# Second attention in fp32: one full-precision product of probabilities and values becomes three rounded ones, with the sums copied by VectorE

## The chip, the cores and the metric

The kernel runs on one core of one Trainium2 chip. The time is that of the whole kernel in device microseconds. Engines: PE is TensorE (PEld its weight loads), ACT ScalarE, DVE VectorE, POOL GpSimd, and SP the queue that issues nearly all DMAs.

## The reference, cut to what matters

The program is two transformer-like blocks, one after the other. The change lies in the attention of the second block (`mla_mixer`), 8 heads, 1024 queries, 1040 keys (16 of them "meta" keys), with a mask by chunks of 64 positions:

```
s = jnp.einsum('bqhd,bkhd->bhqk', qb, k).astype(jnp.float32) * scale
mask = cid[None, :] <= qc[:, None]
s = jnp.where(mask[None, None], s, neg)
p = jax.nn.softmax(s, axis=-1).astype(v.dtype)
return jnp.einsum('bhqk,bkhd->bqhd', p, v)
...
return o * jax.nn.silu(z)
```

Everything is fp32. After it `h = h + y @ w_out` ends the program.

## The kernel before

Each engine has one program, written out by hand; engines meet only through semaphores. `Steps` counts the steps that an engine has finished, and `w.wait_ge(*act_at.at("exp", h, u))` makes an engine wait for one of them. An engine works strictly in its order, so whatever stands behind a waiting instruction waits as well.

Nearly all matrix products of the kernel are made in a split form: an fp32 operand is rounded to fp32r (its high part), the remainder (fp32 minus high part) is rounded as well (its low part), and high by high, low by high and high by low are summed in PSUM. The product of probabilities and values is the exception: there both operands are plain fp32, and each such matmul runs as two passes (`x2` in the trace).

`attend_pe` goes through 8 heads of 14 units. A unit `(hf, x, c0)` is one block `x` of 128 keys (the last has 16) against one half `hf` of the queries, without the masked columns: 512 columns wide in 6 units of a head, 448, 320 and 192 in two each, and 64 in two (one with 16 keys). In each unit PE does

1. `scores(h, u)`: three fp32r products into one of three "unit" banks (0 to 2),
2. `values(j - 2)`: the fp32 product of the unit two before into the bank of its half (3 or 4), of `vm` (values of two heads with a block of ones between them, so that the sums of probabilities come out beside the result) and `pt`,
3. a step of preparation for the next head: turns of queries and keys (units 0 to 3), the 14 products for the row maxima (`max`, two in each of units 4 to 10) and the turn of the maxima (unit 11), through banks 5 to 7. In head 7 the preparation is gone and the input `y` of the last projection is turned instead.

ACT takes the exponential of a unit into one of four buffers `pt`, copies queries and keys to their high parts `qh` and `kh`, and copies sums and results from PSUM (`summed`: `den`, `og`). DVE makes the low parts `ql` and `kl`, the maxima (TENSOR_REDUCE), the reciprocals of the sums (`inverse`, 4 for each half of a pair of heads), and writes the shift of the next head into `qh`. POOL only multiplies result, gate and reciprocal (`z o` and `y`), 4 instructions for each pair of heads. `kl` has to be made before its bank can take a maxima product, and the shift before the next head's scores.

The last projection (`output_pe`, 8 panels of 128 columns, `pe_dense`) takes its input parts `k` in the order 6, 7, 2, 3, 4, 0, 1, 5. For each, `y_high_act` writes the high part into `XH`, `y_low_dve` the low part into `XL`. Parts 6, 7, 2, 3, 4 are split during head 7 (`early`), parts 0, 1 and 5 of the first half at its end. Part 5 is the result of the last pair of heads.

Of the kernel before, what the change touches and what calls it, by code (L numbers as in the profile page):

```python
# [15 lines left out]
NB = 8  # L16
NMETA = 16
# [128 lines left out]
def build(nc, ap, ctx):  # L146
# [3369 lines left out]
    pts = [X(f"pt{i}", 37888 + 2048 * i, [512]) for i in range(4)]  # L3516
# [27 lines left out]
    def values_of(h, x):  # L3544

        return vm[0:n_keys(x), x, h // 2, h % 2:h % 2 + 2, :]
# [102 lines left out]
    def attend_pe(pe, w):  # L3649
# [10 lines left out]
        def values(j):  # L3660
            h, u = j // nu, j % nu
            hf, x, c0 = units[u]
            if x == 0:
                take(w, "values", ("o", h, hf), (act_at, ("o", h, hf)))
            w.wait_ge(*act_at.at("exp", h, u))
            w.wait_ge(*pool_la.at("ones"))
            pe.matmul(tile("o", h, hf)[:, c0:512], values_of(h, x), pts[j % 4][0:n_keys(x), 0:512 - c0], start=(x == 0), stop=(x == last_x[hf])  # L3667
                      ).then_inc(*pe_at.up("values", j))

        for h in range(8):  # L3670
            for u in range(nu):
                scores(h, u)
                if nu * h + u >= 2:
                    values(nu * h + u - 2)
                if h < 7:
                    for step in prepare[u]:
                        prepare_pe(pe, w, h + 1, *step)
                elif u < 4:
                    y_turn_pe(pe, w, *early[u])
        values(8 * nu - 2)  # L3680
        values(8 * nu - 1)

    def attend_act(act, w):
        def summed(h, hf):
# [5 lines left out]
            act.activation(den[hf][a:a + 64, :], p[b:b + 64, :], ACT.Copy).then_inc(*act_at.up("den", h, hf))  # L3690
            act.activation(og[hf][a:a + 64, :], p[a:a + 64, :], ACT.Copy).then_inc(*act_at.up("o", h, hf))

        for h in range(8):
            for u in range(nu):
                hf, x, c0 = units[u]
                j = nu * h + u
                w.wait_ge(*pe_at.at("unit", h, u))
                if j > 3:
                    w.wait_ge(*pe_at.at("values", j - 4))
                act.activation(pts[j % 4][0:n_keys(x), 0:512 - c0], tile("unit", h, u)[0:n_keys(x), 0:512 - c0], ACT.Exp).then_inc(*act_at.up("exp", h, u))  # L3700
                if u == 2 and h > 0:
# [392 lines left out]
```

## Time and profile before

| what | value |
|---|---|
| median of 3 runs | 1920.88 us (1919.63 to 1922.67) |
| the profiled execution's own time | 1921.68 us |
| its span | 1919.9 us |
| second attention, first score product to first product of the last projection | 1656.3 to 1829.25 us |
| last projection to the end | 1829.25 to 1919.9 us |
| PE busy over the span | 1858.6 us (97%) |
| DVE, ACT, POOL busy over the span | 1188.0, 783.2, 553.2 us |

An average over the span says nothing of a stage: the change lies in 173 us of it, so those are read by head, by wait and by single instructions. A start time minus the one before it is the price of a matmul on PE; the durations shown of matmuls overlap.

### The profile page before, as it was taken

The page shows a single profiled execution, that of the slowest core. Times are in us where ns is not written, and L with a number is a line of the kernel's source. Part 1 is how long each engine was busy: PE and PEld are TensorE (multiplying, and loading weights), DVE is VectorE, ACT ScalarE, POOL GpSimd, SP SyncE. Part 2 cuts the span into 40 slices and gives each one's busy share as a digit, 9 for nine tenths or more (in the row PEclk, how much of TensorE's full clock was granted, in tenths as well). Part 3 has the DMA queues.
Part 4 walks back from the last instruction along what each step waited for, and adds up shares of the span by engine and source line. Part 5 has one row for each costly group of instructions (what it writes and reads, how often), then busy time and mean ns, then how long its engine had stood idle before and what let it go on. Part 6 is the DMA issues. An engine that isn't in the chain of part 4 may idle for free.

```text
span 1919.9 us, 24216 instructions
## 1 busy us (share of the span) xinstructions
PE 1858.6 (97%) x9462; PEld 1511.5 (79%) x9462; DVE 1188.0 (62%) x1805; ACT 783.2 (41%) x1404; POOL 553.2 (29%) x555
## 2 busy tenths in 40 slices
PE   8999999899988999999999998999999999999999
PEld 5788788666777888887888887879988897676687
DVE  6678445555788676767877877455435347666642
ACT  6765323455543333433333354452211137455520
POOL 0120026440537666620000024551523125111100
PEclk9999999999999999999999999999999999999999
DMA  4143433300314535469555500113101313411131
GB/s 161 44 148 105 148 89 105 110 23 34 132 56 159 175 127 180 138 263 398 210 191 189 206 1 29 47 59 132 45 23 34 121 45 140 129 34 34 45 131 66
DMA packets 110042, 216.27 MB, mean 113 GB/s; under 512 B 37528, under 2 KB 42904, under 8 KB 105832
## 3 DMA queue, kind: packets, MB, share of 16 engines
q1 hardware_dynamic: 109640, 214.49, 32.8%
q8 instruction: 75, 1.23, 0.3%
q14 instruction: 39, 0.32, 0.1%
q10 hardware_dynamic: 288, 0.22, 0.0%
HBM read 153.82 MB, written 60.87 MB: 112 GB/s over the span
## 4 chain that ended last, share of the span: by engine, by line
PE 74%; DVE 10%; ACT 6%; POOL 4%; issue 3%; DMA 2%; SPq 0%; DVEq 0%; POOLq 0%; ACTq 0%
PE ps L362 10%; PE ps L363 9%; PE ps L364 9%; PE ps L1949 5%; PE ps L1951 5%; PE ps L1950 5%; PE ps L2337 5%; PE ps L2338 5%; PE ps L2339 5%; PE ps L3667 4%; PE ps L379 3%; PE ps L707 2%; ACT sc L1503 1%; PE ps L3568 1%; PE ps L3656 1%
## 5 line engine op out<-in xcount | busy, mean ns | idle before, releaser
L362 PE MATMUL ps<-xh,whi 128*128 128x512 f32 (+2 forms) x1160 | 458.7, 395 | 8.8 <-DVE wlo L331 5.1
L363 PE MATMUL ps<-xl,whi 128*128 128x512 f32 (+2 forms) x1160 | 443.8, 383 | 0.0
L364 PE MATMUL ps<-xh,wlo 128*128 128x512 f32 (+2 forms) x1160 | 442.9, 382 | 0.0
L362 PEld LDWEIGHTS ps<-xh,whi 128*128 128x128 f32 x1160 | 220.5, 190 | 58.2 <-issue 11.5
L364 PEld LDWEIGHTS ps<-xh,wlo 128*128 128x128 f32 x1160 | 220.5, 190 | 40.0
L363 PEld LDWEIGHTS ps<-xl,whi 128*128 128x128 f32 x1160 | 220.6, 190 | 33.2
L1949 PE MATMUL ps<-oph,wsh 128*128 128x512 f32 x448 | 177.2, 396 | 11.2 <-DVE stu L2067 6.0
L2337 PE MATMUL ps<-dnh_b,dnh_a 128*128 128x512 f32 x448 | 175.2, 391 | 4.7 <-DVE dn_b L2363 4.7
L1950 PE MATMUL ps<-opl,wsh 128*128 128x512 f32 x448 | 176.4, 394 | 0.0
L1951 PE MATMUL ps<-oph,wsl 128*128 128x512 f32 x448 | 176.3, 393 | 0.0
L2338 PE MATMUL ps<-dn_b,dnh_a 128*128 128x512 f32 x448 | 174.9, 390 | 0.0
L2339 PE MATMUL ps<-dnh_b,dn_a 128*128 128x512 f32 x448 | 174.8, 390 | 0.0
L2354 ACT ACTIVATE dnh_a<-dnr_a 128x2048 fp32r<-128x2048 f32 x28 | 53.7, 1918 | 188.9 <-PE ps L2339 174.9
L319 ACT ACTIVATE whi<-wraw 128x1024 fp32r<-128x1024 f32 x71 | 74.3, 1046 | 135.6 <-PE ps L364 124.3
L331 DVE TENSOR_TENSOR wlo<-wraw,whi 128x1024 fp32r<-128x1024 f32 x70 | 95.1, 1359 | 55.6 <-ACT whi L319 55.5
L1949 PEld LDWEIGHTS ps<-oph,wsh 128*128 128x128 f32 x448 | 85.5, 191 | 30.6 <-DVE stu L2067 6.5
L2337 PEld LDWEIGHTS ps<-dnh_b,dnh_a 128*128 128x128 f32 x448 | 84.5, 189 | 23.1 <-DVE dn_b L2363 5.4
L1951 PEld LDWEIGHTS ps<-oph,wsl 128*128 128x128 f32 x448 | 85.4, 191 | 17.9
L1950 PEld LDWEIGHTS ps<-opl,wsh 128*128 128x128 f32 x448 | 85.5, 191 | 17.8
L2339 PEld LDWEIGHTS ps<-dnh_b,dn_a 128*128 128x128 f32 x448 | 84.4, 188 | 17.7
L2338 PEld LDWEIGHTS ps<-dn_b,dnh_a 128*128 128x128 f32 x448 | 84.5, 189 | 17.4
L3667 PE MATMUL ps<-pt,vm 128*128 128x512 f32 (+4 forms) x224 | 89.8, 485 | 0.9 <-ACT pt L3700 0.9
(516 smaller groups left out, 3397.7 us busy)
## 6 DMA issues: line engine op xcount, KB each, us to landing
wraw<-panels SPq DMA_DIRECT2D x70, 512.0 KB, 3.6
dnr_b<-ff_d SPq DMA_DIRECT2D x28, 1024.0 KB, 7.6
dnr_a<-down SPq DMA_DIRECT2D x28, 1024.0 KB, 5.1
ff_d<-st SPq DMA_DIRECT2D x64, 256.0 KB, 5.9
ff_d<-stt SPq DMA_DIRECT2D x48, 256.0 KB, 5.9
upx<-up SPq DMA_DIRECT2D x16, 512.0 KB, 3.9
upy<-up SPq DMA_DIRECT2D x16, 512.0 KB, 5.5
hT<-x SPq DMA_DIRECT2D x8, 512.0 KB, 5.1
```

The lines of the kernel that those rows point to most:

```text
L319: act.activation(whi[b][:, 0:n], raw[b][:, 0:n], ACT.Copy).then_inc(*act_w.up(i))
L331: dve.tensor_tensor(wlo[b][:, 0:n], raw[b][:, 0:n], whi[b][:, 0:n].bitcast(F32), ALU.subtract).then_inc(*dve_w.up(i))
L362: pe.matmul(out, h, xh[:, xk, c0:c1_], start=(n == 0), stop=False)
L363: pe.matmul(out, h, xl[:, xk, c0:c1_], start=False, stop=False)
L364: mm = pe.matmul(out, l, xh[:, xk, c0:c1_], start=False, stop=(n == nk - 1))
L1949: pe.matmul(out, h, opH[i][:, j], start=(i in FIRST_UP and j == 0), stop=False, skip_group_check=i not in FIRST_UP)
L1950: pe.matmul(out, h, opL[i][:, j], start=False, stop=False, skip_group_check=i not in FIRST_UP)
L1951: mm = pe.matmul(out, l, opH[i][:, j], start=False, stop=(j == 3), skip_group_check=i not in FIRST_UP)
L2337: pe.matmul(out, h[:, j, cs], xh[:, j], start=(i in (1, 5, 6, 7) and j == 0), stop=False, skip_group_check=i in (2, 3, 4))
L2338: pe.matmul(out, h[:, j, cs], xl[:, j], start=False, stop=False, skip_group_check=i in (2, 3, 4))
L2339: mm = pe.matmul(out, l[:, j, cs], xh[:, j], start=False, stop=(j == 3), skip_group_check=i in (2, 3, 4))
L3667: pe.matmul(tile("o", h, hf)[:, c0:512], values_of(h, x), pts[j % 4][0:n_keys(x), 0:512 - c0], start=(x == 0), stop=(x == last_x[hf])).the ...
```

## The change

The product of probabilities and values is made of three fp32r products as the others are.

- Values: `value_high_act` (ACT) and `value_low_pool` (POOL) split the values of each pair of heads, `vhs`/`vls`, two buffers. The first pair is split at the start of the stage, pairs 1 to 3 in units 5 (ACT) and 6 (POOL) of heads 0, 2 and 4.
- Probabilities: ACT takes the exponential twice, once into `ph` (fp32r, six buffers) and once into `pt` (fp32, now three buffers). POOL subtracts them into `pl` (four buffers). One `pt` is free again when POOL has subtracted, one `ph` and `pl` when PE has done the third product.
- PE: `values_high(j - 2)` (two products), and `values_low(j - 4)` (the third) follow the scores of a unit.
- `summed` moves from ACT to DVE, and to units 4 and 12 (was 2 and 7). The reciprocals of a pair of heads now all stand in the even head behind it, units 0 to 3 and 5 to 8 (were in units 10 to 13 of the odd head and 3 to 6 of the even one).
- POOL's `gated` and `divided` stand between its subtractions, and for the last pair behind all of them.
- In head 7 `early` starts at unit 4 (was 0). All loads of `hr` (the last sum's other operand) are issued after the attention; three stood ahead of it. They also come behind a weight panel's load.

```diff
+    def value_high_act(act, w, c):
+        if c == 0:
+            w.wait_ge(*pe_la.at("mz", 3, HALF2))
...
+        for n, bs in value_parts:
+            act.activation(vhs[c % 2][0:n, bs, 0:3:step, :], vm[0:n, bs, c, 0:3:step, :], ACT.Copy).then_inc(*act_at.up("vh", c, n))
...
+    def value_low_pool(pool, w, c):
+        if c == 0:
+            w.wait_ge(*pool_la.end())
...
+        for n, bs in value_parts:
+            w.wait_ge(*act_at.at("vh", c, n))
+            pool.tensor_tensor(vls[c % 2][0:n, bs, 0:3:step, :], vm[0:n, bs, c, 0:3:step, :], vhs[c % 2][0:n, bs, 0:3:step, :].bitcast(F32), ALU.subtract).then_inc(*pool_at.up("vl", c, n))
...
+        def values_high(j):
...
+            w.wait_ge(*act_at.at("exp high", h, u))
+            w.wait_ge(*pool_at.at("vl", c, NMETA))
...
+        def values_low(j):
...
+            w.wait_ge(*pool_at.at("p low", j))
...
-                if nu * h + u >= 2:
-                    values(nu * h + u - 2)
+                if j >= 2:
+                    values_high(j - 2)
+                if j >= 4:
+                    values_low(j - 4)
...
+                act.activation(p_high(j)[0:n, 0:512 - c0], p, ACT.Exp).then_inc(*act_at.up("exp high", h, u))
+                if j > 2:
+                    w.wait_ge(*pool_at.at("p low", j - 3))
+                act.activation(pts[j % 3][0:n, 0:512 - c0], p, ACT.Exp).then_inc(*act_at.up("exp", h, u))
...
+        for n in range(4):
+            inverse(3, 0, n)
+        summed(7, 1)
+        for n in range(4):
+            inverse(3, 1, n)
         for k in (0, 1, 5):
             if k > 0:
                 w.wait_ge(*pe_at.end())
             y_low_dve(dve, w, k, 0)
-        for n in range(4):
-            inverse(3, 1, n)
...
+                w.wait_ge(*act_at.at("exp", h, u))
+                if j > 3:
+                    w.wait_ge(*pe_at.at("values", j - 4))
+                pool.tensor_tensor(p_low(j)[0:n, 0:512 - c0], pts[j % 3][0:n, 0:512 - c0], p_high(j)[0:n, 0:512 - c0].bitcast(F32), ALU.subtract
+                                   ).then_inc(*pool_at.up("p low", j))
```

What the change makes of two places in the programs. First DVE, from the first split of `y` in head 7 to the splits for the second half of the projection, before:

```order
L3646 TENSOR_TENSOR xl<-ps,xh 128x512 x4
L3646 TENSOR_TENSOR xl<-zf_305,xh 128x512 x6
L3718 RECIPROCAL den_353<-den_353 128x128 x4
L3646 TENSOR_TENSOR xl<-yb,xh 128x512 x2
L3646 TENSOR_TENSOR xl<-zf_305,xh 128x512
L3718 RECIPROCAL den_354<-den_354 128x128 x4
L3646 TENSOR_TENSOR xl<-yb,xh 128x512 x2
```

and now:

```order
L3687 TENSOR_TENSOR xl<-ps,xh 128x512 x4
L3687 TENSOR_TENSOR xl<-zf_305,xh 128x512 x4
L3772 COPY den_375<-ps 64x512
L3773 COPY og_373<-ps 64x512
L3687 TENSOR_TENSOR xl<-zf_305,xh 128x512 x2
L3778 RECIPROCAL den_375<-den_375 128x128 x4
L3772 COPY den_376<-ps 64x512
L3773 COPY og_374<-ps 64x512
L3778 RECIPROCAL den_376<-den_376 128x128 x4
L3687 TENSOR_TENSOR xl<-yb,xh 128x512 x2
L3687 TENSOR_TENSOR xl<-zf_305,xh 128x512
```

Behind the splits of `early`, two copies and four reciprocals of the second half now stand ahead of the low parts of `yb` (parts 0 and 1), which were ahead of them.

Then POOL in units 3 to 8 of head 4, where before it had only four multiplications (`zf<-zf,og` and `zf<-zf,den`) in the whole head; now:

```order
L3826 TENSOR_TENSOR pl_357<-pt_347,ph_353 128x192
L3826 TENSOR_TENSOR pl_354<-pt_345,ph_348 128x64
L3816 TENSOR_TENSOR zf_305<-zf_305,den_375 128x512
L3826 TENSOR_TENSOR pl_355<-pt_346,ph_349 128x512
L3826 TENSOR_TENSOR pl_356<-pt_347,ph_350 128x512
L3587 TENSOR_TENSOR vl_370<-vm,vh_368 128x8x2x64
L3587 TENSOR_TENSOR vl_370<-vm,vh_368 16x2x64
L3826 TENSOR_TENSOR pl_357<-pt_345,ph_351 128x512
L3810 TENSOR_TENSOR zf_305<-zf_305,og_374 128x512
L3826 TENSOR_TENSOR pl_354<-pt_346,ph_352 128x512
```

The four multiplications and the split of the next pair's values stand between the subtractions on whose result PE's third product waits.

## Rows read from the trace of the kernel before

**Rows 1.** The page, busy time, share of the span and instructions.
```profile
PE 1858.6 (97%) x9462; PEld 1511.5 (79%) x9462; DVE 1188.0 (62%) x1805; ACT 783.2 (41%) x1404; POOL 553.2 (29%) x555
```
**Rows 2.** Busy time by stretch: heads 2, 5, 7.
```profile
1700.20:1722.20 22.00, 21.70 (x104) 15.40 (x103) 16.46 (x29) 11.51 (x23) 3.82 (x3) 1.00 0.16 37
...
1765.90:1787.80 21.90, 21.63 (x104) 15.32 (x102) 11.92 (x22) 11.47 (x24) 1.27 (x1) 1.00 0.00 1
...
1809.70:1829.30 19.60, 19.60 (x93) 13.73 (x91) 11.10 (x15) 14.97 (x31) 1.72 (x2) 1.00 0.00 1
```
**Rows 3.** Waits in the stretch 1655 to 1835 (total, times, longest).
```profile
ACT pt L3700 <- PE ps L3658: 69.2, 67, 1.7
...
PE ps L3568 <- DVE kl L3593: 1.9, 7, 0.3
```
**Rows 4.** The chain that ended last, in order of time.
```profile
1690.29 0.86 PE ps L3667 x2
```
**Rows 5.** Timeline of PE: start, duration, line.
```profile
1755.36 0.39 PE L3656 MATMUL ps<-qh,kh 120*128 120x512 f32 x1
1755.59 0.39 PE L3657 MATMUL ps<-ql,kh 96*128 96x512 f32 x1
...
1764.47 0.28 PE L3657 MATMUL ps<-ql,kh 96*128 96x192 f32 x1
1764.58 0.27 PE L3658 MATMUL ps<-qh,kl 96*128 96x192 f32 x1
```
**Rows 6.** POOL by line and form: busy us, mean ns.
```profile
L1630 POOL TENSOR_TENSOR xl<-gat,xh 128x512 fp32r<-128x512 f32 x8 | 10.2, 1280 | 26.7 <-ACT xh L1616 26.7
...
L3125 POOL TENSOR_TENSOR cnv<-cnv,f 128x1024 f32<-128x1024 f32 x2 | 4.9, 2456 | 10.0 <-DVE f L2808 10.0
...
L1198 POOL TENSOR_TENSOR tk<-tk,c 128x64 f32<-128x64 f32 x8 | 2.6, 323 | 0.0
```
**Rows 7.** Timeline of the start of the stage.
```profile
1657.09 1.06 ACT L3252 ACTIVATE zf<-zf 128x1024 f32<-128x1024 f32 x1 [5.39 <-DVE zf L2808]
...
1657.71 1.04 POOL L3383 CAST qh<-aq 24x1024 fp32r<-24x1024 f32 x1
...
1660.11 1.12 PE L3667 MATMUL ps<-pt,vm 128*128 128x512 f32 x2 [0.89 <-ACT pt L3700]
```
**Rows 8.** Timeline of PE around a long wait in an earlier stage.
```profile
608.04 0.80 PE L1949 MATMUL ps<-oph,wsh 128*128 128x512 f32 x1 [6.03 <-DVE stu L2067]
608.63 0.63 PE L1950 MATMUL ps<-opl,wsh 128*128 128x512 f32 x1
...
613.32 0.43 PE L1949 MATMUL ps<-oph,wsh 128*128 128x512 f32 x1
```
**Rows 9.** DVE by line and form: copy from PSUM.
```profile
L1548 DVE COPY sc<-ps 128x512 f32<-128x512 f32 x14 | 9.7, 690 | 2.6 <-PE ps L379 2.4
```
**Rows 10.** Timeline of ACT in head 7.
```profile
1818.09 0.60 ACT L3700 ACTIVATE pt<-ps 128x512 f32<-128x512 f32 x1 [0.35 <-PE ps L3658]
...
1818.59 0.62 ACT L3641 ACTIVATE xh<-zf 128x512 fp32r<-128x512 f32 x1
...
1820.76 0.59 ACT L3690 ACTIVATE den<-ps 64x512 f32<-64x512 f32 x1
...
1821.38 0.59 ACT L3691 ACTIVATE og<-ps 64x512 f32<-64x512 f32 x1
```
**Rows 11.** Timeline of the end of head 7 and the start of the projection.
```profile
1825.41 3.38 DVE L3718 RECIPROCAL den<-den 128x128 f32<-128x128 f32 x4
...
1828.82 2.39 DVE L3646 TENSOR_TENSOR xl<-yb,xh 128x512 fp32r<-128x512 f32 x2
1828.87 1.78 POOL L3747 TENSOR_TENSOR zf<-zf,den 128x512 f32<-128x512 f32 x1 [5.54 <-DVE den L3718]
```
**Rows 12.** Timeline in head 2: DVE and POOL at the same time.
```profile
1702.87 0.75 DVE L3598 SCALAR_TENSOR_TENSOR ql<-ps,vec,qh 96x512 fp32r<-96x512 f32 x1
...
1702.92 1.28 POOL L3747 TENSOR_TENSOR zf<-zf,den 128x512 f32<-128x512 f32 x1 [9.40 <-DVE den L3718]
```
**Rows 13.** The page, DMA issues: KB each, us to landing.
```profile
hT<-x SPq DMA_DIRECT2D x8, 512.0 KB, 5.1
```

More of the change, by code:

```diff
@@ L3689, in summed @@
                 w.wait_ge(*pool_at.at("y", h // 2 - 1, hf))
[L3690 to L3701, printed above, removed]
-                    summed(h - 1, 1)
-                if u == 7:
-                    summed(h, 0)
-                if h < 7:
-                    for step in prepare[u]:
-                        prepare_act(act, w, h + 1, *step)
-                elif u < len(early):
-                    y_high_act(act, w, *early[u])
-        for k in (0, 1, 5):
-            y_high_act(act, w, k, 0)
-        summed(7, 1)
-    def attend_dve(dve, w):
+            dve.tensor_copy(den[hf][a:a + 64, :], p[b:b + 64, :]).then_inc(*dve_at.up("den", h, hf))
+            dve.tensor_copy(og[hf][a:a + 64, :], p[a:a + 64, :]).then_inc(*dve_at.up("o", h, hf))
         def inverse(c, hf, n):
             d = den[hf][:, 128 * n:128 * n + 128]
-            w.wait_ge(*act_at.at("den", 2 * c + 1, hf))
+            w.wait_ge(*dve_at.at("den", 2 * c + 1, hf))
             dve.reciprocal(d, d).then_inc(*dve_at.up("inverse", c, hf, n))
@@ L3724, in attend_dve @@
                         prepare_dve(dve, w, h + 1, *step)
[L3725 to L3730 removed]
+                if h > 0 and h % 2 == 0 and u < 4:
+                    inverse(h // 2 - 1, 0, u)
+                if u == 4 and h > 0:
+                    summed(h - 1, 1)
+                if h > 0 and h % 2 == 0 and 5 <= u < 9:
+                    inverse(h // 2 - 1, 1, u - 5)
+                if u == 12:
+                    summed(h, 0)
+                if h == 7 and 4 <= u < 4 + len(early):
+                    y_low_dve(dve, w, *early[u - 4])
+        for n in range(4):
[3 more added lines that the diff above has]
+            inverse(3, 1, n)
         for k in (0, 1, 5):
@@ new lines, in divided @@
+        def divided(c, hf):
+            z = zf2[:, c, 512 * hf:512 * hf + 512]
+            w.wait_ge(*dve_at.at("inverse", c, hf, 3))
+            w.wait_ge(*pool_at.at("z o", c, hf))
+            pool.tensor_tensor(z, z, den[hf][:], ALU.mult).then_inc(*pool_at.up("y", c, hf))
+        value_low_pool(pool, w, 0)
+        for h in range(8):
+            for u in range(nu):
+                hf, x, c0 = units[u]
+                j, n = nu * h + u, n_keys(x)
+                w.wait_ge(*act_at.at("exp", h, u))
[3 more added lines that the diff above has]
+                                   ).then_inc(*pool_at.up("p low", j))
+                if h % 2 == 0 and h < 6 and u == 6:
+                    value_low_pool(pool, w, h // 2 + 1)
+                if h > 0 and h % 2 == 0:
+                    if u == 0:
+                        gated(h // 2 - 1, 0)
+                    if u == 4:
+                        divided(h // 2 - 1, 0)
+                    if u == 7:
+                        gated(h // 2 - 1, 1)
+                    if u == 10:
+                        divided(h // 2 - 1, 1)
@@ L3864, in sp_program @@
         w.wait_ge(*st_h1.end())
-        for n in range(3):
-            sp.dma_start(hr[n][:], h1_d[n]).then_inc(*ld_hr[n].up())
         sp_weights(sp, w, OUT0 + 3)
         w.wait_ge(*pe_at.end())
-        for n in range(3, 8):
+        for n in range(8):
             sp.dma_start(hr[n][:], h1_d[n]).then_inc(*ld_hr[n].up())
```

105 lines of the change are left out of this document (77 added, 28 removed).

## The prediction

> **What bounds the kernel now.** I read the page first. PE is busy 97% of the span [rows 1], so the first question is whether PE is also the limit inside the stretch that is changed. The busy time by stretch says yes: of the 22.0 us of head 2 PE is busy 21.70, of the 21.9 of head 5 21.63, and in head 7 it never rests [rows 2]. A head takes 21.9 us, and in it ACT works 11.5 us, DVE 16.5 in even heads (those with reciprocals) and 11.9 in odd ones, POOL at most 3.8. The waits confirm it from the other side: ACT stood 69.2 us in all for PE's scores, while the largest wait of PE's products was 1.9 us in 7 times, for `kl` [rows 3]. So every microsecond taken from PE here counts until another engine is the limit, and the other three have, per head of 21.9, about 10 (ACT), 5 to 10 (DVE) and 18 (POOL) us to give. The change takes little from PE and gives much to the three.
>
> **The change part by part.** All in us, against the profiled execution.
>
> *PE's work.* A full fp32 product of values (two passes, 512 columns) takes 0.86 on the chain [rows 4]. An fp32r product of 512 columns comes 0.23 after the one before it, one of 192 columns 0.11 [rows 5], so a narrow one costs no less than its weight load. Three products cost 0.70 (512 columns), 0.33 (192) and 0.33 (64). Scaled with the columns from 0.86, the fp32 product costs 0.77, 0.54, 0.33, 0.22 for 448, 320, 192, 64. Between the rows, three fp32r products cost 0.62 and 0.44 for 448 and 320. A head saves 6 x 0.16 + 2 x 0.15 + 2 x 0.10 + 2 x 0 - 2 x 0.11 = 1.3, eight heads **10.3**. PE then needs 20.6 for a head.
>
> *The start.* PE's first product of values began at 1660.1, when ACT's first exponential was done, after a wait of 0.9 [rows 7]. Now it needs the low values of the first pair. POOL is busy until 1658.75 (its copy at 1657.71), ACT ends its gate at 1658.15 [rows 7] and then splits 1536 elements, about 1.4 if 512 take 0.5 [rows 10], until about 1659.6. POOL's subtraction of 1536: a two-operand POOL instruction takes 1.28 for 512 and 2.46 for 1024 [rows 6], so 3.6, and 0.6 for the 16 meta rows (192 elements, between 0.32 for 64 and 1.28). PE can go on at about 1663.9: **+3.8**, an idle PE of some 4.8.
>
> *What idleness does to the clock.* At 601.6 to 608.0 PE waited 6.03 us, and the 12 matmuls after it came 0.43 apart, 5.28 for what takes 2.8 at 0.23 [rows 8]: that is the lower of the two clock levels, 1.2 in place of 2.4 GHz, and it cost 2.5. For the shorter wait at the start I take **+1.0**, since PE's slower products there partly run while it would wait for POOL anyway.
>
> *POOL in the heads.* 14 subtractions in a head, the same operation as the first line of [rows 6]: 6 x 1.31 + 2 x (1.17 + 0.88 + 0.59) + 2 x 0.30 = 13.8, with a few hundredths between two. That is under 20.6. But head 0 has the split of the second pair in one piece behind unit 6, 3.6 + 0.6 = 4.2, while a low part has only about two units of slack (it is made some 3 us after the scores, and used four units later, 5.9 us): I take **+1.7** for PE in units 11 to 13. Heads 2 and 4 have 13.8 + gaps 0.5 + four multiplications 5.2 + a split of 1024 and 128 elements 2.8 = 22.3: more than PE's 20.6, so the saving is gone, **+1.7** each. In heads 3 and 5 ACT's copies of keys stand behind exponentials that wait for POOL's backlog, and `kl`, for which PE already waits, comes later: **+1.25** each. Their bounds are 0 and about 2.6, the wait of one long POOL piece handed on twice.
>
> *DVE in the heads.* Four copies of 64x512 from PSUM: 0.69 each by a copy of the same length [rows 9], 2.8 a head; and four more reciprocals (0.845 each, [rows 11]) in even heads: 16.5 + 2.8 + 3.4 = 22.7 of durations, about a tenth less by their distance on the engine. So even heads are at DVE's limit too. In heads 2 and 4 this lies beside POOL's; in head 6, without a split, I take **+0.7**. In sum +6.6 in heads 1 to 6; odd head 1 follows a head without reciprocals and costs nothing.
>
> *ACT in the heads.* +14 exponentials, about 5.5 by a spacing of 0.50 at 512 columns, -2.4 for the sums: 14.6 of 20.6. Not the limit, except in head 7: there each unit is two exponentials and a split of `y`, 3 x 0.50 = 1.5 [rows 10], against PE's 1.4, and DVE's low parts read two SBUF operands while POOL subtracts: **+1.3**, that is, head 7 keeps its 18.7 to 19.
>
> *The end.* This is the largest term. DVE's order, as the part on the change shows it, puts behind the attention: one or two low parts 1.2, eight reciprocals 6.8, two copies 1.2, and only then the low part 0, 0.7: about 9.9 us after PE's last value product. PE has five of eight parts ready, 15 products, 3.5. It waits 6.4. Next to POOL's multiplications the low parts of `yb` took 2.39 for two in place of 1.38 [rows 11], so low parts 0 and 1 each come later by up to 0.5: **+7.0**. Before, the same low parts came at 1828.82 and nothing waited. That wait is as long as the one of [rows 8] and is followed by full-width products: **+2.5** for the clock.
>
> *The loads of `hr`.* Issued behind the split of a panel, some 13 us after the attention, 5.1 us to landing [rows 13]. DVE's first evacuation waits for it, but PE has four banks, two panels or 22 us of products plus its own stall, so it is hidden with some 8 us to spare. If it were not, each us late is a us.
>
> Sum: -10.3 + 3.8 + 1.0 + 1.7 + 6.6 + 1.3 + 7.0 + 2.5 = **+13.6**. On the profiled execution's 1921.7 (its span 1919.9 and 1.8 around it) that is 1935.3; this execution is 0.8 above the median of its three runs, so I forecast **1934.5**.
>
> **A rule weighed against the rows.** While POOL's multiplication ran at 1702.92 in its usual 1.28, DVE made a `ql` (one operand in PSUM, one in SBUF) at 1702.87 in its usual 0.75 [rows 12]: no contention. With two SBUF operands there was some: POOL 1.78 and DVE 2.39 for two [rows 11]. The sum goes by these rows.
>
> The Trainium skill ("SBUF — State Buffer", section "SBUF: two separate sides") says that DVE with two SBUF inputs and GpSimd reading SBUF share one port pair under an exclusive lock, and that the one who comes second is blocked for the whole instruction of the other. The trace agrees in which instructions collide. By the rule in full, a low part at the end could wait for a whole 1.3 us multiplication, which would make the sum some 0.7 larger.
>
> **The rivals.**
> 1. *The heads keep up* (0.15). The lag of POOL is absorbed by the buffers, and heads 1 to 6 run at PE's 20.6. For it: the mean POOL work over two heads is 18, below 20.6. Against it: a low part has only four units before PE needs it, and a `pt` three. Then 13.6 - 6.6 - 1.7 = +5.3: 1926.
> 2. *ACT becomes the limit of the middle* (0.15). Two activations that read the same bank might not overlap: `den` and `og`, from one bank, were 0.62 apart and not 0.50 [rows 10]. Then a unit's pair costs 0.12 to 0.24 more, 2 to 3 a head, and copies of keys come later by as much in every head; about +1 a head over my sum: +20, 1941.
> 3. *POOL slower beside DVE* (0.12). If the reductions and copies of DVE also stretched POOL, say by the 15% between 1.28 and the 1.5 or so of a half overlapped pair, POOL has 25 in heads 2 and 4 and 4.8 at the start: +6.6 more, 1941.
> 4. *The other side: a full fp32 product costs PE more than its 0.86* (0.04), in that the next weight load can't run under its second pass. If 0.2 us of each of the 112 were hidden in the products around them, 22.4 more would be saved: 13.6 - 22.4 = -8.8, 1912. It decides from 13.6 / 112 = 0.12 us a product on. Against it: the starts of 0.23 in [rows 5] leave no such room.
> 5. *The wait at the end does not come* (0.04), because DVE's reciprocals get done before PE is: they can't start before DVE has the last `early` splits, so only if head 7 were held up by others long enough. Then -9.5 and head 7 longer: about +4, no change or slightly slower.
>
> The main case has 0.50.
>
> **How the numbers follow.** A measurement of this kernel tells some 0.2%, 3.8 us. Main case, own range 1930 to 1940 (start 3 to 5, heads 3 to 10, end and clock 7 to 11). The range goes from rival 1 to rivals 2 and 3: 1925 to 1945. Faster holds rival 4, 0.04; within 0.2% the fifth and the edge of the first, 0.06; slower the rest, 0.90.
>
> **What the new profile would show.** Products of values: 336 of fp32r, three in 0.70. PE idle once for 4 to 5 us at about 1660, then once for 6 to 7 us some 3.5 us after the first product of the last projection, followed by 7 to 12 products 0.43 apart. Head periods: about 26 for head 0, 20.5 for head 1, 22 for 2 and 4, 21.5 for 3 and 5. POOL busy some 120 us more, nearly without rest in heads 2 and 4. Wrong would be: heads of 20.6 throughout (POOL and DVE are hidden), heads of 23 or more (rivals 2, 3), or a projection that starts without a wait.

## The result: 0.8% slower, and the profile after

The changed kernel takes 1936.54 us (median of 4 runs, 1933.89 to 1937.24) against 1920.51 for the kernel before (4 runs). The ratio is 1.008, with a 95% interval from 1.0068 to 1.0092. The forecast was 1934.5, in a range from 1925 to 1945.

Its profiled execution has a span of 1934.9, against 1919.9: +15.0. The page's busy times of the changed kernel answer to [rows 1]:

```profile
PE 1856.5 (96%) x9574; PEld 1529.1 (79%) x9574; DVE 1209.4 (63%) x1837; ACT 809.3 (42%) x1492; POOL 674.6 (35%) x675
```

PE has 112 more matmuls and is busy 2 us less, part of it at half the clock. POOL has 121 us more. Such totals don't say where 15 us went. For that I took the start of every head's first score product from the timeline of PE, in both traces. All distances are in us.

| stretch | before | after | difference |
|---|---|---|---|
| start of the stage (work that is the same in both) | 1656.33 | 1657.18 | +0.85 |
| head 0 | 21.93 | 27.53 | +5.60 |
| heads 1 to 6 | 22.02 21.82 22.02 21.82 22.02 21.82 | 20.93 21.81 21.45 21.81 21.40 21.66 | -2.46 |
| head 7 | 19.47 | 20.14 | +0.67 |
| last projection to the end | 90.65 | 100.99 | +10.34 |

The start of the stage lies between 1653.8 and 1658.8 in the traces of this study, though nothing ahead of it differs, so the first line is scatter. The middle of the stage gained 2.5, its two ends lost 16.6. The heads don't all hold the same work: the third product comes four units late, so head 0 makes ten of them and head 7 eighteen. That moves about 0.5 from the first head to the last (a kernel below with fp32 in heads 0 and 7 has 20.42 in head 1, which takes nothing over, and 19.95 in head 7 against 19.47).

The waits and the busy time by stretch name the causes. The waits of PE and of the engines that feed it in the changed kernel, from 1655 to 1860, answer to [rows 3] (total, times, longest):

```profile
ACT ph L3750 <- PE ps L3699: 37.5, 56, 1.6
POOL pl L3826 <- ACT pt L3753: 26.0, 34, 2.3
...
ACT pt L3753 <- POOL pl L3826: 9.7, 12, 1.9
...
PE ps L362 <- DVE xl L3687: 7.9, 1, 7.9
...
PE ps L3710 <- POOL vl L3587: 4.6, 1, 4.6
...
PE ps L3609 <- DVE kl L3634: 2.5, 7, 0.6
PE ps L3609 <- DVE nmx L3648: 1.6, 3, 0.6
PE ps L3718 <- POOL pl L3826: 1.5, 4, 0.6
```

PE has one wait at each end, for POOL's split of the first pair's values and for DVE's low part of `yb`, and small ones in the heads. Before, it waited 0.89 at the start, and the largest wait in the heads was 0.3. Busy time by stretch of the changed kernel, answering to [rows 2] (heads 2, 5, 7), and then the two ends. Behind the stretch stand its length, the busy time of PE, PEld, DVE, ACT and POOL with their instructions, and last the granted clock, the DMA share and GB/s:

```profile
1705.64:1727.45 21.81, 20.97 (x118) 17.21 (x117) 19.73 (x34) 14.93 (x34) 17.84 (x18) 1.00 0.16 37
1770.35:1791.75 21.40, 20.71 (x117) 17.18 (x117) 13.54 (x25) 14.21 (x35) 16.66 (x18) 1.00 0.00 1
1813.77:1833.91 20.14, 19.50 (x109) 16.05 (x108) 12.01 (x14) 17.26 (x40) 16.18 (x17) 1.00 0.00 1
1657.20:1664.60 7.40, 2.86 (x17) 2.31 (x18) 1.43 (x2) 6.65 (x10) 6.35 (x6) 0.83 0.41 107
1664.60:1668.00 3.40, 3.39 (x12) 2.83 (x13) 1.34 (x2) 2.22 (x6) 3.11 (x4) 0.50 0.00 0
1833.90:1845.50 11.60, 3.71 (x16) 2.74 (x15) 11.47 (x15) 2.62 (x4) 4.82 (x4) 0.75 0.00 0
1845.50:1849.50 4.00, 3.95 (x9) 2.65 (x9) 4.00 (x5) 0.63 (x1) 1.10 (x1) 0.50 0.00 0
```

In head 2 DVE is now busy 19.73 of 21.81 and POOL 17.84. Behind both long waits the granted clock is 0.50, that is 1.2 GHz: PE works without rest there and gets half as much done. Where PE stood at the end, DVE was busy 11.47 of 11.60. The timeline of DVE in the changed kernel shows with what:

```profile
1834.37 2.39 DVE L3687 TENSOR_TENSOR xl<-zf,xh 128x512 fp32r<-128x512 f32 x2
1836.68 3.38 DVE L3778 RECIPROCAL den<-den 128x128 f32<-128x128 f32 x4
1840.09 0.69 DVE L3772 COPY den<-ps 64x512 f32<-64x512 f32 x1
1840.81 0.69 DVE L3773 COPY og<-ps 64x512 f32<-64x512 f32 x1
1841.53 3.39 DVE L3778 RECIPROCAL den<-den 128x128 f32<-128x128 f32 x4
1844.84 2.31 DVE L3687 TENSOR_TENSOR xl<-yb,xh 128x512 fp32r<-128x512 f32 x2
```

These are the instructions that the prediction summed up for the end. PE's timeline shows the wait (it stands behind the row) and then products 0.43 apart, later 0.24:

```profile
1845.52 0.79 PE L362 MATMUL ps<-xh,whi 128*128 128x512 f32 x1 [7.91 <-DVE xl L3687]
...
1848.64 0.63 PE L362 MATMUL ps<-xh,whi 128*128 128x512 f32 x1
1849.07 0.63 PE L363 MATMUL ps<-xl,whi 128*128 128x512 f32 x1
...
1849.89 0.39 PE L362 MATMUL ps<-xh,whi 128*128 128x512 f32 x1
1850.13 0.40 PE L363 MATMUL ps<-xl,whi 128*128 128x512 f32 x1
```

### The profile page after: what moved, and what is told of

Read it like the earlier page. It is cut to its first block, busy times and chain, and to the rows that moved or that the text cites. A ratio compares the mean times of both kernels' runs of the same rounds, so it can differ in the third digit from the quotient of the medians.

```text
span 1934.9 us, 24802 instructions
## 1 busy us (share of the span) xinstructions
PE 1856.5 (96%) x9574; PEld 1529.1 (79%) x9574; DVE 1209.4 (63%) x1837; ACT 809.3 (42%) x1492; POOL 674.6 (35%) x675
## 3 DMA queue, kind: packets, MB, share of 16 engines
q8 instruction: 76, 1.25, 0.3%
## 4 chain that ended last, share of the span: by engine, by line
PE 70%; DVE 13%; ACT 7%; POOL 5%; issue 4%; DMA 2%; SPq 0%; DVEq 0%; POOLq 0%; ACTq 0%
PE ps L362 10%; PE ps L363 9%; PE ps L364 9%; PE ps L2337 5%; PE ps L2339 5%; PE ps L2338 5%; PE ps L1949 5%; PE ps L1950 4%; PE ps L1951 4%; PE ps L379 2%; PE ps L707 2%; ACT sc L1503 1%; PE ps L3609 1%; DVE fm L1156 1%; DVE den L3778 1%
## 5 line engine op out<-in xcount | busy, mean ns | idle before, releaser
L3826 POOL TENSOR_TENSOR pl<-pt,ph 128x512 fp32r<-128x512 f32 (+4 forms) x112 | 108.7, 983 | 33.6 <-ACT pt L3753 26.0
L2337 PEld LDWEIGHTS ps<-dnh_b,dnh_a 128*128 128x128 f32 x448 | 84.8, 189 | 22.3 <-DVE dn_b L2363 4.8
L2338 PEld LDWEIGHTS ps<-dn_b,dnh_a 128*128 128x128 f32 x448 | 84.8, 189 | 17.8
```

The lines of the kernel that those rows point to most:

```text
L2337: pe.matmul(out, h[:, j, cs], xh[:, j], start=(i in (1, 5, 6, 7) and j == 0), stop=False, skip_group_check=i in (2, 3, 4))
L2338: pe.matmul(out, h[:, j, cs], xl[:, j], start=False, stop=False, skip_group_check=i in (2, 3, 4))
L3826: pool.tensor_tensor(p_low(j)[0:n, 0:512 - c0], pts[j % 3][0:n, 0:512 - c0], p_high(j)[0:n, 0:512 - c0].bitcast(F32), ALU.subtract).then_i ...
```

## The experiments

The theory was that of the prediction: PE saves about one us a head, both ends of the stage lose more by what POOL and DVE have to do first, and in heads 2 and 4 these two engines eat the saving. Its rivals were those of the prediction. The kernel before ran in every batch; its medians were 1920.65 to 1921.11.

### The end: order of DVE behind head 7

```diff
-                if u == 12:
+                if u == (9 if h == 7 else 12):
                     summed(h, 0)
+                if h == 7 and u >= 10:
+                    inverse(3, 0, u - 10)
...
-        for n in range(4):
-            inverse(3, 0, n)
-        summed(7, 1)
-        for n in range(4):
-            inverse(3, 1, n)
         for k in (0, 1, 5):
...
             y_low_dve(dve, w, k, 0)
+        summed(7, 1)
+        for n in range(4):
+            inverse(3, 1, n)
```

> DVE's order at the end alone is changed: the sums of head 7's first half are copied in unit 9, its four reciprocals stand in units 10 to 13, and the low parts of y 0, 1 and 5 stand ahead of the copies and reciprocals of the second half. My theory (the wait of 7.9 us in the projection and the 1.2 GHz products behind it come from eight reciprocals and two copies ahead of low part 0): the wait shrinks to under 2 us, perhaps as one short wait in the second half of the first panel, no product runs at 1.2 GHz, the stretch from the first product of the projection to the end falls from 101.0 to 91 to 93 us, the whole to 1927 to 1929. Rival (the loads of hr, now behind the attention, hold the projection): it stays near 101. The stage of attention stays at 176.7.

Measured: 1930.90, ratio to the kernel before 1.0052 (1.0035 to 1.0069). The order behind head 7 alone is worth 5.6 us, or about 0.3% of the kernel. The projection takes 96.4 in place of 101.0, and the waits of PE, from 1655 to 1860, are now:

```profile
PE ps L3710 <- POOL vl L3587: 4.6, 1, 4.6
PE ps L362 <- DVE xl L3687: 4.4, 4, 2.1
```

The longest of the four is 2.1, at 1835.86, and the products behind it are 0.23 to 0.24 apart: in this trace the clock stayed at 2.4 GHz. (A run below had the same wait and did not keep the clock.) The direction is as expected and rules out the rival that the loads of `hr` alone set the projection; the size missed, 96.4 in place of 91 to 93 and 1930.9 in place of 1927 to 1929. Of what is left, 96.4 - 90.65 = 5.7, the waits are 4.4. They belong to DVE, which still has the copies and interleaves reciprocals with low parts.

### The start: the first pair's low values on DVE

```diff
+    def value_low_dve(dve, w):
+        w.wait_ge(*pool_la.end())
+        for n, bs in value_parts:
+            w.wait_ge(*act_at.at("vh", 0, n))
+            dve.tensor_tensor(vls[0][0:n, bs, :, :], vm[0:n, bs, 0, :, :], vhs[0][0:n, bs, :, :].bitcast(F32), ALU.subtract).then_inc(*dve_at.up("vl", 0, n))
...
-        value_low_pool(pool, w, 0)
+        w.wait_ge(*pool_la.end())
```

> Only the low part of the first pair's values moves from POOL to DVE, which is idle there for 5 us. My theory (PE's 4.6 us wait at the start is ACT's split and then POOL's 3.5 + 0.6): DVE needs about 1.8 + 0.3, PE's wait falls to about 2.5, head 0 from 27.5 to about 25.5, and perhaps fewer products at 1.2 GHz behind it; the whole 2 to 3 us less, 1934. Rival (the exponentials behind ACT's split set the start): head 0 stays at 27, no change.

Measured: 1934.66, ratio 1.0071 (1.0056 to 1.0086), 1.9 less than the changed kernel; head 0 takes 25.15 in place of 27.53. The split in POOL's timeline of the changed kernel (start, duration):

```profile
1660.50 3.97 POOL L3587 TENSOR_TENSOR vl<-vm,vh 128x1536 fp32r<-128x1536 f32 x2 [0.91 <-ACT vh L3574]
```

The same two pieces on DVE in this kernel, by line from 1655 to 1670 (busy us, mean ns):

```profile
L3593 DVE TENSOR_TENSOR vl<-vm,vh 128x1536 fp32r<-128x1536 f32 (+1 forms) x2 | 2.0, 1049 | 2.6 <-ACT vh L3574 2.6
```

And PE's wait in this kernel:

```profile
PE ps L3716 <- ACT ph L3756: 2.6, 1, 2.6
```

POOL takes 3.97 for the two pieces, DVE 2 x 1.05 = 2.1. PE's wait falls from 4.55 to 2.58, as expected, but does not go. It changes its owner: it is now for ACT's first exponential, which stands behind the split of the high values (1.72) and the load of ACT's table (1.28, also there before the change). The timeline of ACT in this kernel:

```profile
1658.89 1.72 ACT L3574 ACTIVATE vh<-vm 128x1536 fp32r<-128x1536 f32 x2
1660.62 1.28 ACT L3756 ACT_TABLE_LOAD   x1
1661.91 0.60 ACT L3756 ACTIVATE ph<-ps 128x512 fp32r<-128x512 f32 x1
```

### The heads: subtraction and reciprocal shortened, each alone and both

These three kernels leave out part of the work. The first leaves out POOL's subtraction beyond 64 columns of each tile, from unit 9 of head 0 to the end of head 6; the second leaves out the reciprocals of 112 of every 128 columns in the first three pairs; the third has both edits.

```diff
+                c0 = 448 if 9 <= j < 7 * nu else c0
                 pool.tensor_tensor(p_low(j)[0:n, 0:512 - c0], pts[j % 3][0:n, 0:512 - c0], p_high(j)[0:n, 0:512 - c0].bitcast(F32), ALU.subtract
```
```diff
-            d = den[hf][:, 128 * n:128 * n + 128]
+            d = den[hf][:, 128 * n:128 * n + (16 if c < 3 else 128)]
```

> Leaves out part of the work: from unit 9 of head 0 to the end of head 6 POOL subtracts only 64 columns of each unit, all other instructions and waits are kept. My theory (in heads 2 to 5 PE waits for POOL's low parts, and through pt and ACT for kl): periods of heads 2 to 5 fall from 21.81, 21.45, 21.81, 21.40 to about 21.2, 20.6, 21.2, 20.6, the whole by 3 to 5 us, 1932. Rival (DVE alone limits them): they stay within 0.2.

> Leaves out part of the work: reciprocals of the first three pairs of heads on 16 of 128 columns each, about 0.7 us less for each of 24. If DVE limits the even heads, heads 2, 4 and 6 fall from 21.8 to about 20.7, the whole by 3 us. My theory (POOL in heads 2 and 4, DVE only in head 6): heads 2 and 4 fall by 0.4, head 6 by 0.9, the whole by 1 to 2 us, 1935; heads 3 and 5 unchanged.

> Leaves out both: GpSimd subtracts only 64 columns of each probability tile from head 0's unit 9 to the end of head 6, and the reciprocals of the first three pairs cover 16 of 128 columns. Theory A (heads 2 and 4 are held by GpSimd and VectorE together, each alone being enough; heads 3 and 5 by GpSimd's backlog): heads 2, 4 and 6 fall from 21.8, 21.8, 21.7 to 20.9, as head 1 has, heads 3 and 5 to 20.9, and the attention from its first product of scores on becomes 3.5 to 4 us shorter than in the changed kernel, against 1.8 with the subtraction alone and 0.6 with the reciprocals alone. Rival (the third cause is ScalarE's two exponentials or PE's own products): heads 2 and 4 stay at 21.4 or more. If head 1's 20.9 is itself PE's own need and not a wait, no head falls under 20.8; by my prediction's price of three products it would be 20.6.

| kernel | median | ratio and interval | heads 1 to 6 |
|---|---|---|---|
| changed | 1936.54 | 1.0080 (1.0068 to 1.0092) | 20.93 21.81 21.45 21.81 21.40 21.66 |
| short subtraction | 1934.65 | 1.0069 (1.0054 to 1.0084) | 20.91 21.65 20.92 21.66 20.96 21.65 |
| short reciprocal | 1933.72 | 1.0068 (1.0053 to 1.0083) | 20.93 21.77 21.43 21.82 21.40 21.03 |
| both | 1933.04 | 1.0060 (1.0046 to 1.0074) | 20.90 21.09 20.99 21.02 20.95 21.03 |

The medians of the three differ by no more than the runs scatter, so the head periods decide. Heads 3 and 5 fell to 20.9 with POOL's work alone: they were held by POOL's backlog. Head 6 stood at 21.65 with POOL's and fell to 21.03 with DVE's alone: it was held by DVE. Heads 2 and 4 stood at 21.65 to 21.82 with either edit, and fell to 21.0 to 21.1 only with both: each of the two engines was enough to hold them. Both single expectations missed in heads 2 and 4, which I had expected to fall by 0.6 and 0.4, and which fell by 0.16 at most. In the waits of PE (1655 to 1860) the releaser changes with the edit. With the short subtraction:

```profile
PE ps L3609 <- DVE nmx L3648: 1.6, 3, 0.6
```

With the short reciprocal:

```profile
PE ps L3718 <- POOL pl L3826: 2.0, 6, 0.6
```

In the first PE still waits 0.55 for `nmx` once in each of heads 2, 4 and 6, as in the changed kernel. In the second these waits are gone, and in heads 2 and 4 waits for `pl` have come instead. Of the third's expectation the heads came true, the size did not: heads 1 to 6 together are 3.1 shorter, but the attention only 2.4 (174.4 against 176.7) and not 3.5 to 4. Head 0 took 28.22 in place of 27.53 there, because the low clock behind its wait lasted longer (last section), and the edits of this kernel come only behind that.

### Repairs together, and fp32 kept in some heads

Three kernels, all of which also moved reciprocals into the odd heads. For that, the copies of an odd head's first half had to move ahead, to unit 9:

```diff
-                if h > 0 and h % 2 == 0 and u < 4:
-                    inverse(h // 2 - 1, 0, u)
+                if h % 2 == 1 and h < 7 and u >= 10:
+                    inverse(h // 2, 0, u - 10)
...
-                if u == 12:
+                if u == (9 if h % 2 else 12):
                     summed(h, 0)
```

The second and third keep the fp32 product in the heads of `PLAIN`, heads 0 and 7 in the second, 0, 2, 4, 6 and 7 in the third. In both, the first pair's values are split inside head 0, and the copies of head 7's first half stand in unit 7:

```diff
+            if h in PLAIN:
+                w.wait_ge(*act_at.at("exp", h, u))
...
+                pe.matmul(tile("o", h, hf)[:, c0:512], vm[0:n, x, c, h % 2:h % 2 + 2, :], pts[j % 3][0:n, 0:512 - c0], start=(x == 0), stop=(x == last_x[hf])
+                          ).then_inc(*pe_at.up("values", j))
+                return
```

> Complete computation. The end of head 7 as in the run with the changed end order (first half's copies in unit 9, its reciprocals in units 10 to 13, low parts 0, 1 and 5 ahead of the last copies and reciprocals), the first pair's low values on VectorE, and the first half's reciprocals of pairs 0 to 2 moved from the even heads to units 10 to 13 of the odd ones. If the first two add up: 1936.5 - 5.6 - 1.9 = 1929. The third gives heads 2, 4 and 6 up to 3.4 us of VectorE back, but GpSimd alone still holds heads 2 and 4 at 21.6 to 21.8, and heads 3 and 5 get the reciprocals: between -1 and +1 us. Expected 1928 to 1930. Rival (VectorE is the only limit in even heads): heads 2 and 4 fall to 21 and the time is 1926 or less.

> Complete computation. Heads 0 and 7 keep the fp32 product of probabilities and values, heads 1 to 6 have the three rounded ones; VectorE copies the sums everywhere, the end has the changed order, the reciprocals of the first halves are in the odd heads. Theory (a head saves what PE saves, 1.0, less what GpSimd and VectorE hold back; the losses of the change lie in the two ends): no wait for low values at the start, head 0 at 22, heads 1 to 6 at 20.9, 21.8, 21.6, 21.8, 21.6, 21.2, head 7 at 19.3, hence -2.5 us in the heads, and the start and the last projection as in the kernel before: 1917 to 1920. Rival (the change's loss at the last projection comes from the loads or from VectorE's copies, not from the order behind head 7): the projection stays 5 us or more longer and the time is over 1923.

> Complete computation. As the run with fp32 in heads 0 and 7, but only heads 1, 3 and 5 have the three rounded products; heads 0, 2, 4, 6 and 7 keep the fp32 one. Theory (GpSimd holds even heads because multiplications, the next pair's split and 14 subtractions fall together there; VectorE likewise): odd heads all run at head 1's 20.9, even heads at PE's 22.0, so 3 x 1.0 = 3 us are saved, and the ends are as before: 1917 to 1919, no worse than with six such heads. Rival (head 1's 20.9 was owed to a lag caught up from head 0, not to the products): odd heads at 21.4 or more and no gain, 1920 or more.

| kernel | median | ratio and interval | heads 1 to 6 | projection |
|---|---|---|---|---|
| three repairs | 1932.14 | 1.0058 (1.0044 to 1.0072) | 22.12 21.88 22.62 21.87 22.60 21.14 | 96.4 |
| fp32 in heads 0 and 7 | 1926.09 | 1.0027 (1.0018 to 1.0036) | 21.61 21.88 22.62 21.84 22.57 21.14 | 93.5 |
| products in heads 1, 3, 5 | 1924.72 | 1.0021 (1.0013 to 1.0030) | 21.61 22.70 21.62 22.69 21.61 22.69 | 93.6 |

All three missed their expectation, by 2 to 6 us. In the second and third the projection accounts for 2.9 of that. In the heads the reason is one that I had not seen: where the repairs put the copies. In the first kernel the odd heads became 1.2 longer than in the changed kernel. The waits of PE in the second kernel (1655 to 1860):

```profile
PE ps L379 <- DVE nms L3656: 2.3, 3, 0.8
```

DVE's timeline at the end of its head 3:

```profile
1737.36 0.68 DVE L3784 COPY den<-ps 64x512 f32<-64x512 f32 x1
1738.08 0.70 DVE L3785 COPY og<-ps 64x512 f32<-64x512 f32 x1
1738.80 0.77 DVE L3650 TENSOR_REDUCE nmx<-ps 128x1 f32<-128x512 f32 x2
1739.61 0.18 DVE L3656 TENSOR_REDUCE nms<-nmx 128x8 f32<-128x24 f32 x1
1739.71 0.94 DVE L3790 RECIPROCAL den<-den 128x128 f32<-128x128 f32 x1
1740.68 1.23 DVE L3660 TENSOR_TENSOR qh<-ps,aq 8x1024 fp32r<-8x1024 f32 x1
```

And the timeline of PE there, the turn of the maxima and the next head's first score product:

```profile
1739.94 0.29 PE L379 MATMUL ps<-ident,nms 128*104 128x128 f32 x1 [0.77 <-DVE nms L3656]
...
1742.06 0.47 PE L3699 MATMUL ps<-qh,kh 120*128 120x512 f32 x1
```

The two copies stand ahead of the last reduction for the maxima, and PE's turn of the maxima waits 0.8 for it. Then a reciprocal stands ahead of the shift (L3660), and the next head's first score product starts right behind the shift, at 1742.06. Behind the maxima, in unit 12, the same copies made no such wait. So the three runs don't speak against the theory of POOL and DVE, but they can't support it either. The third has a second lesson: the low products come four units late, so those of an odd head's last four units are paid in the even head behind it. With a wait of 0.22 for `nmx` on top, an even head with fp32 took 22.7 and not 22.0. The projection was 2.9 longer than before, with three waits of 0.66 to 0.78 for DVE's low parts. The changed order alone had left 5.7 of the 10.3 lost there. How much of the further 2.8 comes from the fp32 product in head 7, and how much from its copies two units earlier, was not separated.

### Both engines relieved

Now DVE and POOL are relieved without putting anything ahead of the maxima: ACT copies the sums again (`summed` with `act.activation`, behind the exponentials of units 4 and 9), and the values of pairs 2 and 3 are split in heads 3 and 5.

```diff
-                if h % 2 == 0 and h < 6 and u == 5:
-                    value_high_act(act, w, h // 2 + 1)
+                if (h, u) in ((0, 5), (3, 5), (5, 5)):
+                    value_high_act(act, w, (h + 1) // 2 if h else 1)
```

One kernel has the three products in all heads; the other also keeps the fp32 product in heads 0 and 7, and the old order of the end.

> Complete computation. The changed kernel with the sums copied by ScalarE and the values of pairs 2 and 3 split in heads 3 and 5; three products in all heads, the start as changed, and at the end the reciprocals still ahead of the last low parts. Theory: heads 1 to 6 at 20.9 to 21.0 (126 in place of 128.7 in the changed kernel), start of head 0 unchanged at 27.5, at the end the two copies of 0.7 are gone from VectorE, so PE's wait falls from 7.9 to about 6.5: 1936.5 - 2.7 - 1.5 = 1932.3. Rival (ScalarE becomes the limit): heads no shorter than in the changed kernel.

> Complete computation. Heads 0 and 7 keep the fp32 product and the whole order of head 7 and of the end as before the change (sums copied by ScalarE, low parts of yb ahead of the last reciprocals), only that the splits of y begin in unit 4. Heads 1 to 6 have the three products; ScalarE copies the sums everywhere, and the values of pairs 2 and 3 are split in heads 3 and 5 in place of 2 and 4. Theory (heads 2 and 4 are held by GpSimd and VectorE together, and both are relieved here): VectorE has 2.8 less in every head, GpSimd 2.8 less in heads 2 and 4, so all of heads 1 to 6 run at the 20.9 to 21.0 which they had with both operations shortened, in sum 125.7 against 131.5 before; start and last projection as before. 1920.8 - 5.5 = 1915.3, range 1913.5 to 1918. Rival (the copies on ScalarE delay the exponentials, ScalarE has then 17 of 21): heads of 21.4 or more and 1918 or more. Rival 2 (the loss in the last projection is the loads of hr behind the attention, which stay there): a projection of 95 or more and no gain.

Three products in all heads: 1931.76, ratio 1.0054 (1.0040 to 1.0067), heads 1 to 6 at 20.93 20.93 20.96 20.88 20.97 20.88, which is what was expected of them. The total came near its 1932.3 in another way than expected: PE's wait at the end fell to 3.3 and not 6.5, head 7 became 1.4 longer, and the projection took 98.7, 2.3 less. With fp32 in heads 0 and 7: 1917.78 (10 runs), ratio 0.9981 (0.9971 to 0.9990), heads 20.42 20.94 20.94 20.88 20.96 20.88, projection 93.1. This beats both kernels; 2.5 were given back in the projection, which I had expected as before. Busy time by stretch in the second, heads 2 and 4:

```profile
1701.10:1722.10 21.00, 20.72 (x118) 17.21 (x118) 16.90 (x29) 16.36 (x37) 17.28 (x18) 1.00 0.17 39
1743.00:1763.90 20.90, 20.61 (x117) 17.16 (x117) 16.89 (x29) 16.57 (x38) 18.58 (x19) 1.00 0.16 39
```

PE is busy all but 0.3, its old wait for `kl`; DVE has 16.9 and ACT 16.4 to 16.6, so ACT did not become the limit. In head 7 of the kernel with three products everywhere it did: 21.57, with three waits of PE for `ph` of about 0.3.

### The loads of `hr`

```diff
-        sp_weights(sp, w, OUT0 + 3)
         w.wait_ge(*pe_at.end())
         for n in range(8):
             sp.dma_start(hr[n][:], h1_d[n]).then_inc(*ld_hr[n].up())
+        sp_weights(sp, w, OUT0 + 3)
```

> Complete computation. The changed kernel with the eight loads of hr issued ahead of the weight panel's load instead of behind it. Theory (the loads are hidden: only VectorE's first evacuation waits for one, and PE has four banks): the same, 1936 to 1937, and PE's waits in the projection are still the single one of 7.9. Rival (the evacuation's wait of 4.6 on VectorE holds up the splits of the next panels and costs PE): 1 us or more is given back.

Measured: 1935.42, ratio 1.0074 (1.0060 to 1.0088). The stage takes 176.8 and the projection 100.9, as in the changed kernel (176.7 and 101.0), with the same single wait of 7.9. DVE's wait for `hr` was 4.6 in the changed kernel and is 4.45 in the fastest one of this study as well. So it costs PE nothing: the order of the loads changed neither stretch by more than 0.1.

### The splits of `y` four units earlier

```diff
+    early_in = [()] * 4 + [(0, 4), (1, 5), (2, 6), (3, 7), (8,), (9,)] + [()] * 4
...
-                    y_high_act(act, w, *early[u - 4])
+                    for i in early_in[u]:
...
+                        y_high_act(act, w, *early[i])
```

DVE's low parts are moved in the same way.

> Complete computation. As the run with the relieved middle, but ScalarE and VectorE make the ten splits of y in head 7 two to a unit in units 4 to 7 and singly in 8 and 9, so that they end four units earlier, where they ended before the change. Theory (what the projection still lost there, 93.1 against 90.65, came from VectorE's lateness: low parts of yb begun 1.4 after the first product of the projection instead of 0.4 before it, and three waits of PE of together 1.7): the waits shrink to 0.5 or less, the projection takes 91 to 91.5, the time is 1916.0 to 1916.5. Rival (the projection's rest is GpSimd's multiplication beside VectorE's low parts, or the loads of hr): the projection stays at 92.5 or more and the time at 1917.8. Rival 2 (two splits in a unit hold up the exponentials): head 7 longer than 20.3.

Measured: 1916.62 (11 runs), ratio 0.9979 (0.9970 to 0.9988). The projection takes 91.8, head 7 19.9 as in the kernel above (so its second rival is out), and of three waits one of 0.8 is left: the theory's direction, with 1.3 of its 1.6 to 2.1. This is the fastest kernel of the study; that it beats the one above is shown by the two traces (projection 91.8 against 93.1, the attention 166.8 and 166.9), not by the two medians, whose intervals overlap.

## Why the prediction was right, step by step

The direction, the range and the size hold (+13.6 forecast on the profiled execution, +15.0 measured). That the sum came so near is in part luck: a saving that was 2.3 too large and heads that were 3.0 too dear cancel.

| term | forecast | measured | read from |
|---|---|---|---|
| PE's saving | -10.3 | -8.0 | 21.92 a head before, 20.92 in heads 2 to 6 with both engines relieved: 1.0 a head |
| wait at the start | +3.8 | +3.7 | 4.55 for `vl`, 0.89 before |
| clock behind it | +1.0 | +1.7 | 3.4 us at 1.2 GHz |
| head 0, split of pair 1 | +1.7 | +0.8 | two waits for `pl`, 0.50 and 0.28 |
| heads 1 to 6 | +6.6 | +3.6 | 129.1 against six of 20.92 |
| head 7 | +1.3 | +1.7 | +0.67 net of a saving of 1.0; some 0.5 of it is work taken over from head 6 |
| wait at the end | +7.0 | +7.9 | the row at 1845.52 |
| clock behind it | +2.5 | +2.0 | 4.0 us at 1.2 GHz |
| loads of `hr` | 0 | 0 | own run |

The measured terms make +13.4; 0.85 is the start of the stage, and 0.8 stays unassigned, about half at each end. (By the low products that come four units late, head 0 saves 1.5 and head 7 only 0.5; the sum is the same, but then about 0.9 of head 0 stays open, and head 7 was held up by 1.2.) The two clock terms are those of this one trace. Other kernels with the same waits had from 3.1 to 5.3 us at 1.2 GHz at the end and up to 9.6 at the start.

**The saving** was mis-sized: 1.0 a head and not 1.3. The prediction's own terms make 1.24 a head and 9.9 in all, not 10.3. The full-width units give what the rows said (unit 9, the one with two maxima products of 400 columns, takes 1.81 in place of 1.97). Six such units at 0.16 are already the whole 1.0, so the eight narrower ones gave nothing in sum, where the scaled prices had put 0.3. **The heads** were too dear by 3.0. For heads 2 and 4 I had summed POOL's durations to 22.3 and taken POOL for the limit. They took 21.8, POOL was busy 17.8 of it in head 2, and the wait that PE had gained there was 0.55 for DVE's `nmx`. The three short kernels showed that either engine alone holds these heads at 21.65 to 21.82; the sum had let DVE's limit lie beside POOL's. Heads 3 and 5 were held as described, through `kl` (0.53 and 0.56 of waiting in place of 0.28), but by 0.5 each and not 1.25. **Head 7** was 19.47 before and not "18.7 to 19". **The start and the end** came as forecast, by the instructions named. At the start the prediction did not see that ACT's own split and table load would hold PE until 1662.6 without POOL.

The low parts at the end cost more than the sum had, but not those that it named. While POOL multiplied, DVE's two from 1834.37 took 2.39, and POOL's from 1834.42 took 1.79:

```profile
1834.42 1.79 POOL L3810 TENSOR_TENSOR zf<-zf,og 128x512 f32<-128x512 f32 x1 [0.80 <-DVE og L3773]
```
```profile
L3687 DVE TENSOR_TENSOR xl<-zf,xh 128x512 fp32r<-128x512 f32 x7 | 8.8, 1298 | 1.2 <-ACT xh L3682 1.0
...
L3687 DVE TENSOR_TENSOR xl<-ps,xh 128x512 fp32r<-128x512 f32 x4 | 2.8, 692 | 3.4 <-ACT xh L3682 3.4
```

The second fence is the view by line of DVE in the stage, changed kernel: with two SBUF operands a low part took 1298 ns on average beside POOL's instructions, with one operand in PSUM 692. Low part 0 itself, for which the prediction had added up to 0.5, was not held up: it began at 1844.84 and PE went on at 1845.52.

The Trainium skill ("SBUF — State Buffer", section "SBUF: two separate sides") says that the first of the two engines has the shared ports for its whole instruction. The trace agrees, if a low part is put at 0.55 of port time: POOL's 1.79 is its usual 1.29 and the 0.5 that DVE's first low part still needed, and DVE's second ended when POOL's 1.79 and its own 0.55 were over, at 1836.76. The prediction put the rule's version of the sum 0.7 higher, for a wait of low part 0. That term came out 0.9 higher, but through the two low parts ahead of the reciprocals (2.39 where the sum had 1.2), so the near match of the two numbers is chance.

**The rivals.** Rival 1 (the heads keep up) is false for this kernel: 21.4 to 21.8 in heads 2 to 6. It became true with both engines relieved. Rival 2 (two activations from one bank don't overlap) is refuted by a row of ACT's timeline; the second starts 0.50 behind the first:

```profile
1737.07 0.60 ACT L3750 ACTIVATE ph<-ps 128x512 fp32r<-128x512 f32 x1 [1.58 <-PE ps L3699]
1737.57 0.59 ACT L3753 ACTIVATE pt<-ps 128x512 f32<-128x512 f32 x1
```

Rival 3 (POOL slower beside DVE's reductions and copies) is refuted by POOL's mean in the same stretch, the 1.28 to 1.29 of before, also for the wide split, where the rows had 2456 (view by line and form):

```profile
L3826 POOL TENSOR_TENSOR pl<-pt,ph 128x512 fp32r<-128x512 f32 x48 | 61.7, 1290 | 24.1 <-ACT pt L3753 23.8
...
L3587 POOL TENSOR_TENSOR vl<-vm,vh 128x1024 fp32r<-128x1024 f32 x2 | 4.8, 2401 | 0.0
```

Rival 4 (the fp32 product costs PE more, so more is saved) has the wrong sign: less was saved than the sum had, 1.0 a head. Rival 5 (no wait at the end) is refuted by the 7.9.

## What to carry to other kernels

A saving on the bounding engine is paid for at the two ends of a stage: what has to be made before its first product, and what the helping engines still have queued behind its last. Here the middle gained 2.5 (6.0 when well arranged, with three products in all heads), the ends lost 16.6, and keeping the old form in the first and the last round, with both helpers relieved between them, turned +0.8% into -0.2%. Before placing a helper's instruction, ask which one behind it has somebody waiting: with two copies ahead of the maxima and a reciprocal ahead of the shift, an odd head took 1.2 us longer. When each of two engines can hold a round, relieving one of them changes nothing and does not clear it; relieve both.

## What the runs showed of the hardware

The length of a wait does not tell how long TensorE works at 1.2 GHz behind it. Behind the wait of 7.9 at the end the changed kernel had 4.0 us at that clock. Four other kernels with a wait of 7.90 to 7.93 at that place had 3.1, 4.0, 5.3 and 5.3. Behind the start's 4.55 it had 3.4. The kernel with both operations shortened, the same up to there, waited 4.56 and then had 9.6, which is why its head 0 took 28.22:

```profile
1662.80:1672.40 9.60, 9.60 (x33) 8.08 (x34) 3.51 (x7) 4.86 (x13) 4.23 (x6) 0.50 0.34 84
```

Behind a wait of 2.10 the kernel with the changed end order kept 2.4 GHz. The one with three repairs had a wait of 2.10 too, and its clock fell about 1 us after it:

```profile
1840.90:1843.90 3.00, 3.00 (x9) 2.30 (x7) 2.94 (x5) 0.66 (x1) 1.28 (x1) 0.50 0.00 0
```

Half of those 3 us, 1.5, stands against 1.2 less of waiting (3.2 in place of 4.4), and its projection took the same 96.4. The kernel with three products in all heads and both engines relieved was at 1.2 GHz twice, for 3.1 us ahead of its wait of 3.3 and for 5.7 behind it:

```profile
1832.10:1835.20 3.10, 3.10 (x9) 2.39 (x8) 3.10 (x5) 0.48 (x1) 0.12 (x1) 0.50 0.00 0
1839.90:1845.60 5.70, 5.65 (x12) 3.97 (x13) 5.18 (x6) 0.80 (x2) 1.09 (x1) 0.50 0.07 4
```

Part of the shorter wait is PE being slow ahead of it. The short subtraction did the same: a wait of 6.3, products 0.43 apart from 1829.94 on, ahead of it, and a projection of 102.0, longer than with the wait of 7.9. So read the granted clock on both sides of a wait before giving the wait a price. And DVE makes the split of 1536 and 192 columns in 2.1 where POOL takes 3.97.
